# Router product in four column strips, second gate's rows behind the output projection, sample's choice and gather moved

## What is computed

```python
def expert_choice_ffn(h, w_router, w_gate, w_up, w_down):
    t = h.reshape(-1, d)
    cap = CAPACITY_FACTOR * n // N_EXPERTS        # 128 of the prompt, 32 of the sample
    aff = jax.nn.softmax((t @ w_router).astype(jnp.float32), axis=-1)
    g, idx = lax.top_k(aff.T, cap)
    xe = t[idx]
    hid = jax.nn.silu(jnp.einsum('ecd,edf->ecf', xe, w_gate)) * jnp.einsum('ecd,edf->ecf', xe, w_up)
    ye = jnp.einsum('ecf,efd->ecd', hid, w_down) * g[..., None].astype(t.dtype)
    out = jnp.zeros_like(t).at[idx.reshape(-1)].add(ye.reshape(-1, d))

def encoder_layer(x, c, ...):
    ...
    x = x + gate1 * mix
    h2 = rms_norm(x, norm_ffn) * (1 + scale2) + shift2
    x = x + gate2 * expert_choice_ffn(h2, ...)
```

## Time and profile before

| | us |
|---|---|
| median of the runs shown | 1611.99 |
| the runs shown | 1600.94, 1611.99, 1614.15 |
| the profiled execution, its time | 1601.3 |
| the profiled execution, its span on the core | 1599.5 |
| TensorE busy in the span | 1474.1 (92%) |
| VectorE busy | 1118.1 (70%) |
| ScalarE busy | 797.3 (50%) |
| share of TensorE in the chain that ended last | 79% |
| share of VectorE in that chain | 8% |

### The profile page before, as it was taken

One profiled execution on the slowest core, in us unless ns is written; L12 is line 12 of the kernel. 1 busy time (PEld: TensorE's weight loads), 2 busy tenths in 40 slices (PEclk: granted clock), 3 DMA queues, 4 the chain that ended last, 5 costly groups with the idle time before them and its releaser, 6 DMA issues.

```text
span 1599.5 us, 27119 instructions
## 1 busy us (share of the span) xinstructions
PE 1474.1 (92%) x10051; PEld 1082.0 (68%) x10051; DVE 1118.1 (70%) x1594; ACT 797.3 (50%) x1306; POOL 175.5 (11%) x207
## 2 busy tenths in 40 slices
PE   3999999799989978998579999999999999999996
PEld 0777787447767756775247777777777777777774
DVE  0258898897767755445848777878777878777874
ACT  1222222127777764222336556666656666656662
POOL 0022112200000000111010111110111110111110
PEclk8999999899999988999679999999999999999998
DMA  8400001361000001321938898888898888898961
GB/s 322 153 11 27 27 1 53 145 265 65 2 1 2 1 1 53 114 111 66 337 129 280 271 319 282 294 280 293 274 314 286 302 273 290 275 313 288 296 201 17
DMA packets 110562, 281.31 MB, mean 176 GB/s; under 512 B 10533, under 2 KB 12681, under 8 KB 107432
## 3 DMA queue, kind: packets, MB, share of 16 engines
q1 hardware_dynamic: 102824, 259.53, 45.5%
q0 software_dynamic: 7680, 20.98, 5.7%
HBM read 259.51 MB, written 20.97 MB: 175 GB/s over the span
## 4 chain that ended last, share of the span: by engine, by line
PE 79%; DVE 8%; ACT 7%; issue 3%; SPq 1%; POOL 1%; DMA 1%; ACTq 0%; DVEq 0%; POOLq 0%
PE banks L1402 11%; PE banks L1377 10%; PE banks L1382 10%; PE banks L1378 10%; PE banks L1076 9%; PE banks L1087 6%; PE banks L1279 6%; PE banks L1227 4%; PE banks L1214 3%; PE banks L1204 3%; ACT xs_t L950 2%; DVE c_t L1602 2%; DVE negmax L1700 2%; PE banks L1302 1%; PE banks L1409 1%
## 5 line engine op out<-in xcount | busy, mean ns | idle before, releaser
L1912 DVE TENSOR_TENSOR low<-raw,high 128x1024 fp32r<-128x1024 f32 x384 | 447.6, 1218 | 1.0
L929 ACT ACTIVATE high<-raw 128x1024 fp32r<-128x1024 f32 x384 | 380.5, 1051 | 3.0 <-PEq L1350 2.2
L1602 DVE SCALAR_TENSOR_TENSOR c_t<-a_t,taps,c_t 128x256 f32<-128x256 f32 (+2 forms) x360 | 215.2, 660 | 0.5
L1377 PE MATMUL banks<-high,x_hi 128*128 128x512 f32 x512 | 208.4, 407 | 0.0
L1378 PE MATMUL banks<-high,x_lo 128*128 128x512 f32 x512 | 200.0, 391 | 0.0
L1382 PE MATMUL banks<-low,x_hi 128*128 128x512 f32 x512 | 158.5, 391 | 1.1 <-DVE low L1912 1.1
L1076 PE MATMUL banks<-h_t,w_in_sb 128*128 128x256 f32 x640 | 142.5, 379 | 1.2 <-DVE h_t L1552 1.2
L1700 DVE TENSOR_REDUCE negmax<-banks 128x1 f32<-128x1024 f32 (+1 forms) x80 | 84.4, 1056 | 68.9 <-PE banks L1204 68.9
L1076 PEld LDWEIGHTS banks<-h_t,w_in_sb 128*128 128x128 f32 x640 | 119.9, 190 | 17.1 <-issue 1.4
L1377 PEld LDWEIGHTS banks<-high,x_hi 128*128 128x128 f32 x512 | 96.0, 188 | 32.9 <-issue 13.6
L1402 PE MATMUL banks<-raw,xs_t 128*32 128x256 f32 x2048 | 117.9, 382 | 0.0
(11 more groups left out here) (216 smaller groups left out, 2183.0 us busy)
## 6 DMA issues: line engine op xcount, KB each, us to landing
raw<-in_w_gate SPq DMA_DIRECT2D x128, 512.0 KB, 4.5
raw<-in_w_up SPq DMA_DIRECT2D x128, 512.0 KB, 5.8
raw<-in_w_down SPq DMA_DIRECT2D x64, 1024.0 KB, 5.0
ada<-in_ada_w SPq DMA_DIRECT2D x24, 1024.0 KB, 7.7
w_in_sb<-in_w_in SPq DMA_DIRECT2D x1, 4096.0 KB, 20.6
x_in<-in_x_prompt SPq DMA_DIRECT2D x4, 1024.0 KB, 4.9
w_out_sb<-in_w_out SPq DMA_DIRECT2D x1, 4096.0 KB, 12.9
x_again<-in_x_prompt SPq DMA_DIRECT2D x4, 1024.0 KB, 5.6
```

The costliest lines, as they stand in the source:

```text
L929: act.activation(high[c % RING][:, :], raw[ph][:, k, :], ACT.Copy).then_inc(hi_ready, 1)
L1377: pe.matmul(bank(b + h), s_hi_k, w_high[:, half], start=(k == 0), stop=False)
L1602: dve.scalar_tensor_tensor(out=c_t[s][:, c, :], in0=a_t[:, c, bass.ds(k + o, n)], scalar=taps[:, c, bass.ds(k, 1)], in1=c_t[s][:, c, :], o ...
L1912: dve.tensor_tensor(low[ph][:, k, :], raw[ph][:, k, :], high[c % RING][:, :].bitcast(F32), ALU.subtract).then_inc(lo_ready, 1)
```

## The change

The router's weights are loaded into `silu_pad`, a tile of 32 columns a row block whose last use as an operand lies before, and the product uses all 32 columns. Row block k goes to strip k mod 4, so that the four strips hold four partial sums on 128 partitions. All 128 are copied, and `turn_logits`, instead of transposing 16 rows, multiplies with `pick`, the sum of the four diagonal pieces of the identity, which adds the strips and turns in one step. The second gate's rows go to banks 0, 6 and 1, directly behind the projection. All four of the sample's rounds stand at round 14, its two float copies behind them, and its transposes and indices have a step of their own, as has its gather on GpSimd. On TensorE the first strips stand ahead of the transposes of the prompt's rows, and VectorE's first two low parts ahead of `x_scale`.

```diff
-    router = keep("router", [P, KC, NE])
+    pick = keep("pick", [P, NE])
...
+    router = silu_pad
...
+            sp.dma_start(router[:, :, 0:NE], w_router[0].rearrange("(k q) e -> q k e", q=P)).then_inc(router_loaded, 16)
             sp.wait_ge(scaled, 2 * CC)
...
+            pool.tensor_tensor(pick[:, :], ident[:, 0:NE], ident[:, STRIP:STRIP + NE], ALU.add).then_inc(pick_made, 1)
+            for j in range(2, 4):
+                pool.wait_ge(pick_made, j - 1)
+                pool.tensor_tensor(pick[:, :], pick[:, :], ident[:, STRIP * j:STRIP * j + NE], ALU.add).then_inc(pick_made, 1)
...
-            pool.wait_ge(top_ready, 5)
...
-            fetch(0, 2)
+            pool.wait_ge(top_ready, 3)
+            pool.tensor_copy(i_now[0:CAP_S, 1:2], i_top_s[0:CAP_S, 0:1]).then_inc(idx_copied, 1)
+            pool.wait_ge(idx_copied, 1)
+            pool.indirect_dma_start(xg_s[:, :], None, xn_s, bass.IndirectOffsetOnAxis(i_now[0:CAP_S, 1:2], axis=0)).then_inc(gathered_s, 16)
+            pool.wait_ge(top_ready, 5)
...
             norm2(2 * NPAIR - 1)
+            act.wait_ge(gate2_made, 1)
+            act.activation(gate2_p[:, 0:512], bank(0), ACT.Copy).then_inc(gate2_ready, 1)
+            act.activation(gate2_p[:, 512:D], bank(6), ACT.Copy).then_inc(gate2_ready, 1)
+            act.activation(gate2_s[:, :], bank(1)[:, 0:D // 4], ACT.Copy).then_inc(gate2_ready, 1)
             h2_out(NPAIR - 1)
...
                 for k in range(KC):
-                    last = pe.matmul(bank(6)[0:NE, 0:2 * P], router[:, k, :], h2_t[:, k, :], start=(k == 0), stop=(k == KC - 1))
+                    j = k % 4
+                    last = pe.matmul(bank(6)[STRIP * j:STRIP * (j + 1), 0:2 * P], router[:, k, :], h2_t[:, k, :],
+                                     start=(k < 4), stop=(k >= KC - 4))
...
-                    last = pe.transpose(bank(7)[:, NE * i:NE * (i + 1)], logits_t[:, P * t:P * (t + 1)], ident[0:NE, 0:NE])
+                    last = pe.matmul(bank(7)[:, NE * i:NE * (i + 1)], logits_t[:, P * t:P * (t + 1)], pick[:, :], start=True, stop=True)
...
             project_out(2 * NPAIR - 1, 1)
 
+            pe.sem_inc(chunk_used, RING)
+            pe.wait_ge(mix_gated, NT - 1)
+            for h in range(2):
+                mod_row(bank((0, 6)[h]), STRIP * (2 + h), 4 + 2 * h, 0, 512)
+            for j in range(4):
+                last = mod_row(bank(1)[STRIP * j:STRIP * (j + 1), 0:256], STRIP * (2 + j // 2) + 1, 4 + j, 256 * (j % 2), 256)
+            last.then_inc(gate2_made, 1)
             pe.wait_ge(aff_copied, 1)
             turn_x1(NPAIR - 1)
+            pe.wait_ge(gate2_ready, 3)
             route(NPAIR - 1)
...
             turn_xs(0)
-            turn_x_rows(0)
             pe.wait_ge(xs_scaled, 1)
             strips(0, 0)
+            turn_x_rows(0)
...
-                    top_eight(aff_s, top_s, idx_s, 0, top_s_step)
-                if r == 15:
-                    top_eight(aff_s, top_s, idx_s, 1, top_s_step)
-            for r in range(2, CAP_S // 8):
-                top_eight(aff_s, top_s, idx_s, r, top_s_step)
+                    for i in range(CAP_S // 8):
+                        top_eight(aff_s, top_s, idx_s, i, top_s_step)
...
+            for c in range(2):
+                split_low(0, c)
             x_scale(0)
```

More of the change, by code:

```diff
@@ L188, in encoder_layer @@
     c_lo = [put(f"c_lo{i}", [P, CC, n], F32R, c_at[i]) for i, (_, n) in enumerate(SPANS)]
-    logits_t = put("logits_t", [NE, TOK], F32, Z2 + 81920)
+    logits_t = put("logits_t", [P, TOK], F32, Z2 + 81920)
+    assert NE <= STRIP
+    router = silu_pad
     HALF = SP_TOK // 2
@@ L260, in encoder_layer @@
         pad_made = sem("pad_made")
+        pick_made = sem("pick_made")
         cols_turned = sem("cols_turned")
@@ L485, in _ @@
                 sp.dma_start(bias_rows[r:r + 4, :], ada_b[0, P * c:P * c + D].rearrange("(b n) -> b n", b=4)).then_inc(bias_rows_loaded, 16)
-            sp.dma_start(router[:, :, :], w_router[0].rearrange("(k q) e -> q k e", q=P)).then_inc(router_loaded, 16)
             for p in range(1, NPAIR):
@@ L627, in _ @@
             pool.sem_inc(ye_free, 1)
-            fetch(0, 2)
+            pool.wait_ge(top_ready, 3)
[3 more added lines that the diff above has]
+            pool.wait_ge(top_ready, 5)
+            pool.tensor_copy(i_now[:, 0:1], i_top_p[:, 0:1]).then_inc(idx_copied, 1)
+            pool.wait_ge(idx_copied, 2)
+            pool.indirect_dma_start(xg_p[:, :], None, xn_p, bass.IndirectOffsetOnAxis(i_now[:, 0:1], axis=0)).then_inc(gathered_p, 16)
             y_s_strips = y_s[0].rearrange("t (j c) -> (t j) c", j=4)
@@ L898, in logits_out @@
                 act.wait_ge(logits_ready, p + 1)
[L899 removed]
+                act.activation(logits_t[:, 2 * P * p:2 * P * (p + 1)], bank(6)[:, 0:2 * P], ACT.Copy).then_inc(logits_copied, 1)
             tile_high(2)
@@ L965, in _ @@
                 split_high(0, c)
[L966 to L969, removed]
             strips_x(0)
@@ L1308, in _ @@
             pe.wait_ge(router_loaded, 16)
+            pe.wait_ge(pick_made, 3)
             for p in range(NPAIR - 1):
@@ L1349, in _ @@
             last.then_inc(aff_turned, 1)
[L1350 to L1356, removed]
+            pe.wait_ge(top_float, 2)
+            for i in range(2):
+                last = pe.transpose(bank(0)[:, NE * i:NE * (i + 1)], top_s4[:, i, :, :].rearrange("e j q -> e (j q)"), ident[0:NE, 0:NE])
+            last.then_inc(top_turned, 1)
             pe.wait_ge(top_float, 4)
             for i in range(2):
[L1359 to L1362, removed]
+                last = pe.transpose(bank(1)[:, RANKED * i:RANKED * (i + 1)], top_p[:, i, :], ident[0:RANKED, 0:RANKED])
             last.then_inc(top_turned, 1)
@@ L1873, in _ @@
                     dve.wait_ge(aff_copied, 2)
[L1874 to L1878 removed]
+                    for i in range(CAP_S // 8):
+                        top_eight(aff_s, top_s, idx_s, i, top_s_step)
+                    dve.wait_ge(top_s_step, 3 * CAP_S // 8)
+                    dve.tensor_copy(top_s4[:, 0, :, :], top_s[:, 0:1, :].to_broadcast([NE, 4, CAP_S])).then_inc(top_float, 1)
+                    dve.tensor_copy(top_s4[:, 1, :, :], idx_s[:, :].unsqueeze(1).to_broadcast([NE, 4, CAP_S])).then_inc(top_float, 1)
             dve.wait_ge(top_p_step, 3 * CAP_P // 8)
[L1880 removed]
             dve.tensor_copy(top_p[:, 1, :], idx_p[:, :]).then_inc(top_float, 2)
[L1882 to L1883 removed]
             dve.wait_ge(top_turned, 1)
[L1885 to L1886 removed]
+            dve.tensor_copy(g_top_s[:, 0:NE], bank(0)[:, 0:NE]).then_inc(top_ready, 1)
             dve.wait_ge(strip_no_made, 4)
[L1888 to L1890 removed]
+            dve.tensor_scalar(i_row_s[:, :], bank(0)[:, NE:2 * NE], 4.0, strip_no[:, 0:1], ALU.mult, ALU.add).then_inc(top_ready, 1)
+            dve.tensor_copy(i_top_s[0:CAP_S, 0:NE], bank(0)[0:CAP_S, NE:2 * NE]).then_inc(top_ready, 1)
+            dve.wait_ge(top_turned, 2)
+            dve.tensor_copy(top_sb[:, :, :], bank(1)[:, 0:2 * RANKED].rearrange("p (i e) -> p i e", i=2)).then_inc(top_copied, 1)
             dve.wait_ge(top_copied, 1)
@@ L1989, in _ @@
             dve.sem_inc(y_p_ready, 1)
-            dve.wait_ge(gate2_ready, 2)
+            dve.wait_ge(gate2_ready, 3)
+            for c in range(2):
+                split_low(0, c)
             x_scale(0)
@@ L1993, in _ @@
             up_strips(0, 0)
-            for c in range(4):
+            for c in range(2, 4):
                 split_low(0, c)
```

11 lines of the change are left out of this document (1 added, 10 removed).

## The result

The changed kernel takes 1593.06 us (median of 8 runs, 1592.12 to 1604.19) where the kernel before took 1610.90 (8 runs, 1600.94 to 1614.15). The ratio is 0.9938, with a 95% interval of 0.9911 to 0.9964: a gain, and of less than 1%. Level against level the gain is 9.5 to 10 us; the two medians lie 18 apart only because more runs of before fell on its upper level.

The account below looks back on a forecast made before the run. TensorE bounds around the output projection, VectorE in the choice rounds. 8.0 + 0 + 2.35 + 1.3 = 11.6 us gained: 1589.7 off the profiled execution, 1600.4 off the median; forecast the middle, 1595, range 1583 to 1606.

Parts of the forecast that it names:

- Term 1: Router products 0 to 2 on TensorE: 0.90 us each in strips instead of 3.56, 8.0 us gained.
- Rival D: Router products: each strip change drains the array, a product takes 6.1 us; 17 us lost, 1618.6; chance 0.05.
- Term 2: Fourth router product and its transposes: faster product, dearer `pick` turn; 0 us, between -0.5 and +2.
- Term 3: The choice rounds: VectorE's 2.66 us wait for the sample's logits goes; +2.35 us, between 1.5 and 3.
- Term 4: Last round to expert 0's first chunk: 5.95 us wait goes, 21.4 us against 22.7; +1.3, between -3 and +5.
- B: Term 4 at its bad end, -3: bare scaling, late landing, half-clock chunk; 7.3 us gained, 1594; chance 0.22.
- C: Second gate's rows, moved behind the projection, fall to half clock, 15.8 us: -3.4; 8.2 gained, 1593; chance 0.06.

Follow-up runs that it names:

- u1: Changed kernel with the router product back in one strip and the logits turned by 16-row transposes again; 1604.02 us, ratio 0.9972.
- d1: Changed kernel with expert 0's down weights loaded only once the prompt's rows are gathered; 1590.06 us, ratio 0.9880.
- u3: Changed kernel with the prompt's transposes ahead of the first strips and VectorE's scaling ahead of its low splits again; 1586.69 us, ratio 0.9877.
- u4: Changed kernel with the prompt's transposes ahead of the first strips on TensorE, VectorE's order left as changed; 1589.65 us, ratio 0.9912.
- u2: Changed kernel with the second gate's rows put back behind the sample's affinities on TensorE, their copies moved back on ScalarE; 1601.49 us, ratio 0.9964.
- g1: Changed kernel with the first gate's four rows each followed by two steps of the next modulation product; 1594.62 us, ratio 0.9925.
- b1: Changed kernel with d2 and g1 together, and the last replacement of the prompt's and sample's choice left out; 1586.00 us, ratio 0.9860.
- d2: Changed kernel with u3 and d1 together; 1588.96 us, ratio 0.9899.

## Why the prediction came out right, and which of its steps did not hold

The predicted 1595 was the middle between two sums, 1589.7 off the profiled execution and 1600.4 off the median, because the text couldn't tell at which level the next median would fall. It fell on the lower, where 1602 less the true gain of 9.5 to 10 gives 1592. That 1595 came within 2 us of the median is in part luck: it lies between the levels, where none of the 8 runs is. The forecast of less than 1% held; the gain was put 2 us too high.

**Term 1** (8.0, measured 7.45). The mechanism holds, as stage 1 of u1 shows by giving back 7.73. The price of a product was 1.00 instead of 0.90, 63 ns a record where the experts' strips take 56. The experts' 48 further records cost 54 ns each ((3.59 - 1.00) / 48), so an estimate is that some 0.14 us are paid once a group, however long it is; what they are is not shown. Rival D, records one behind the other, would have been 6.1. The Trainium skill (TensorE: Matmul & The Clock Gate, Part 3) lets a weight load overlap only where the row group differs, which the prediction priced at 1.2 us as an estimate. The trace does not agree: the product's 16 loads of 109 ns on average, together 1.7 us, lie within the 1.00.

**Term 2** (0, measured -0.43). Product 1.97 (2.1 said), `pick` 3.61 (3.7 said), from the two flip records: 0.47 gained up to there, where 0.2 was said. The turn became dearer not by the width of the logits: the weights have 128 columns in both (L1325 before, L1342 after). It has 16 records where the eight transposes had one each, and it ran at 0.50 where they ran at 1.00. The four transposes behind them, at half clock, took 1.06 instead of 0.63: the text named them and booked 0.2 to balance them, which was too little. And it overlooked the transposes ahead of the product. The first four of the pair took 1.13 (L1306 in the chain of after), against this row in the chain of before:

```profile
733.25 0.67 PE banks L1292 x4
```

There the clock fell at about 734.9, behind them, and in after at about 733.3, ahead of them; this costs 0.47. It is not the strips' doing, since u1 has 1.13 too; what brings the earlier fall is not shown.

**Term 3** (2.35, measured 2.73). The 2.66 went; u1 brings it back as 2.67. What makes up for the 0.3 of the two float copies is VectorE's shorter stall for the sample's `h2`, 0.75 where u1, like before, has 1.21, which the text had not counted.

**Term 4** (1.3, measured -0.25). Here steps failed that partly cancelled. The gate rows ran at 1.00 as said and the 5.95 us wait went. The landing was put at 4.2 with 5.6 at worst, on the reading that the loads "end about then". They did not: the choice now ended while they still ran, and 6.8 lies outside the bound given. d1 measures this step alone: 3.35. On the other side, the gather was issued 1.15 us after the last round and not the 2.1 booked (0.7 and 1.4), since 0.29 us of idle time lie ahead of it where there were 0.93; so the rows came 1.7 later than the sum had them, and not 2.6. The bare scaling was foreseen (4.03 and the turn's 0.7; TensorE idle 3.77), the strips were 5.55 for 6.0, and the slow start was 1.6 for 1.0 (u3). What the text missed is that all this was a choice: it added up the new order without pricing the old one, which, with the gate rows moved, would have given 6 us (u3). The two low splits that it credited to the new order with the 1.08 are a cost in the trace, 1.8 us (u4), and u3, without them there, has no wait of 1.08 either.

**Rivals.** B came near in its mechanism (a late landing, bare scaling, a slow chunk) at a smaller price, -0.25 and not -3. Against C the text set that the first gate's rows keep 1.00. In this kernel they keep it in some executions only, so that row was weaker evidence than it looked, though C did not happen at the new place.

## What to carry to other kernels

When a stall is taken away, ask what the work behind it will now meet: here a gather that had come after the loads came among them, and 3.6 of 5.4 us went there (u2, d1). Hold back a load that nobody needs yet where a small, urgent transfer is about to start. And price each reordering against the old order with the other edits in place: the one that was added to this change cost 6.4 us of what the rest had gained (u3).

## What the runs showed of the hardware

- In these traces a TensorE that is busy without a gap did not always keep or regain its clock. It fell from 1.00 to 0.50 between two equal rows at 344.3 us and stayed there until about 358, for 6.8 us of lost time (after). Rows that began at 338.2 to 338.8 kept 1.00, rows that began at 340.2 to 342.1 did not. The second gate's rows, of the same kind, began at 0.50 before and stayed there for their 16 us; in after they began at 1.00 and kept it for their 8.5 us. What decides it stays open; mixed with other matmuls the first gate's rows kept 1.00 in both profiles taken (g1, b1).
- The same gather of 32 rows took 3.1 to 3.3 us from issue to TensorE when it was issued on idle or nearly idle queues (share 0.00 to 0.16; before, d1, d2, u1, u2) and 6.6 to 6.8 behind weight loads (share about 1.0; after, u3).
- Weights of 128 rows by 32 columns in four strips in turn: 16 records in 1.00 us at full clock and 1.97 at half, against 3.56 at full clock in one strip of 16 columns (5.38 and 6.22 where the clock rose before the product's end).
